# Two transformer blocks of a hybrid model, float32 by split products: the rows of the moving arrays get a pitch of 516 and 514 elements

## The chip, the cores and the metric

One core of a Trainium2 chip runs one program. The metric is the device time of that program in microseconds (us), from its start to its end. Before the change it was run twice: 3772.89 and 3775.09 us, median 3773.99 us.

## The reference

512 tokens of width 1024 go through two blocks of two layers each. Cut to what matters here, one layer of the first block is

```python
h = rms_norm(x, norm_mix[l]);  z = h @ w_in[l]
# attention, a gated recurrence (forward and backward) and a convolution of 31 taps, each on its part of z
x = x + concat([o_att, o_hg, o_cv]) @ w_out[l]
h = rms_norm(x, norm_mlp[l])
x = x + square(relu(h @ w_mlp_in[l])) @ w_mlp_out[l]      # 1024 -> 4096 -> 1024
```

A layer of the second block has the same frame with four mixers, a gate of width 1024 for each, a projection per mixer (512 to 1024) and one output projection, and then the same MLP. All of it is float32, so every large product is computed as three products of rounded parts.

## The kernel before, in words

**Layout.** Activations are kept transposed: partition p and row k of `xT` (128 x 8 x 512) hold feature 128k + p of all 512 tokens. The input of a projection is such an array, split in two of type fp32r (float32 as TensorE takes it in one pass): a high part, the value rounded (`hi = cast(y)`), and a low part, the rest (`lo = y - hi`). The pairs are

- `hH`, `hL` (lines 135 and 136): the normalised input of a layer and, later in the layer, the mixers' outputs, for all layers;
- `H2`, `L2` (lines 1147 and 1148; 1544 in the second block): the input of the MLP;
- `midH`, `midL` (lines 1145 and 1146; 1537 and 1538): the MLP's intermediate, 1024 of its 4096 features at a time;
- `yH`, `yL` (second block, four rows each): the output of one mixer.

Each is allocated by `sb`, which adds bytes behind a tile until its size is a multiple of 128 bytes. A row is 512 elements of 4 bytes, so every row begins 2048 bytes behind the one before it.

**Weights.** They come as a stream of units of 128 x 1024 elements. SyncE loads a unit into one of two slots of `w_raw` (line 257), ScalarE rounds it into `w_hi` (line 233, three slots), and GpSimd computes `w_lo = w_raw - w_hi` (line 280; VectorE does it for some units of the first block, line 249). ScalarE's rounding of a unit waits until the tile that used the slot three units earlier is done.

**Products.** `Group.part` (lines 322 to 345) takes one output tile of 128 features: for k from 0 to 7 it issues three matmuls into one PSUM bank, `w_hi` with the high row k (line 336), `w_lo` with the same high row (line 337), `w_hi` with the low row k (line 338). The activation row is the moving operand, 128 x 512; the weights, 128 x 128, are loaded anew ahead of each matmul. So a tile is 24 matmuls, and each of them reads one row of one moving array and nothing of the next row. `Group.some` (lines 308 to 310) does the same for the first two tiles of the output projection in the first block. Two PSUM banks alternate.

**Around it.** In the MLP the blocks `up0, down0, ... up3, down3` of eight tiles each follow one another. Behind an `up` tile VectorE does four operations in a row (`mlp_dve`, lines 506 to 510): max and scale out of PSUM, square, cast into `midH`, subtract into `midL`. Behind a `down` tile it adds to `xT` (line 371). `scale_dve` (lines 399 and 400) writes the pairs `hH`, `hL` and `H2`, `L2`; lines 1172, 1173, 1468, 1501, 1502, 2239 and 2240 write single rows of `hH` and `hL` from the mixers' outputs. Each of these instructions writes or reads one row as well. Order between engines is kept by semaphores written out by hand; none depends on an address.

Within a layer, arrays of different phases lie at the same addresses: the scopes of `midH`, `midL`, `H2`, `L2` are closed at once, and `Z` and others are laid over them.

Of the kernel before, what the change touches and what calls it, by code (L numbers as in the profile page):

```python
# [16 lines left out]
F32R = mybir.dt.float32r  # L17
# [7 lines left out]
P = 128  # L25
T = 512
NT = T // P
D = 1024
NK = D // P
# [76 lines left out]
def program(nc, given, out):  # L106
# [5 lines left out]
    with ctx:  # L112
        used = {}

        def sb(name, shape, dt=F32, scope=ctx):


            used[name] = used.get(name, 0) + 1
            name = f"{name}_{used[name]}"
            tile = scope.enter_context(nc.sbuf_tensor(name, shape, dt))  # L120
            rest = (-(int(np.prod(shape[1:])) * BYTES[dt]) // 32 * 32) % ALIGN
            if rest:
                scope.enter_context(nc.sbuf_tensor(f"{name}_pad", [P, rest], U8))
            return tile
# [7 lines left out]


        xT = sb("xT", [P, NK, T])
        hH = sb("hH", [P, NK, T], F32R)
        hL = sb("hL", [P, NK, T], F32R)
        rstd = sb("rstd", [P, T])
        w_raw = sb("w_raw", [P, 2, UNIT])
        w_hi = sb("w_hi", [P, WB, UNIT], F32R)
# [68 lines left out]
        def since(s):  # L208


            return begin.get(s.num, 0)
# [206 lines left out]
        def out_pe(layer, early, late, ready, out_tiles=None):  # L418


            begun = out_tiles is not None
            out_tiles = out_tiles or Group(layer, "out")
            for ks in (late,) if begun else (early, late):
                for tile in range(2):
                    out_tiles.some(tile, ks, ready, ks is early, ks is late)
            del out_tiles.tiles[0:2]
            out_tiles.products()
# [24 lines left out]
        def out_dve(layer, y, hi, lo, sq):  # L452
            add_and_scale(2 * layer + 1, Group(layer, "out"), y, hi, lo, sq)

        def h_ready(r):
            return lambda k: pe.wait_ge(h_split, NK * r + k + 1)
# [5 lines left out]

        def mlp_pe(layer, H2, L2, midH, midL, sq, behind=None):
            r = 2 * layer + 1
            for b in range(FB):
                Group(layer, f"up{b}", lambda nk: (H2, L2)).products(
                    ready=h_ready(r) if b == 0 else None,
                    sums=(lambda k: sum_squares(r, sq) if k == NK - 1 else None) if b == 0 else None)
                down = Group(layer, f"down{b}", lambda nk: (midH, midL))
                ready = lambda k, b=b: pe.wait_ge(mid_ready, since(mid_ready) + NK * b + k + 1)  # L470
                if b < FB - 1 or behind is None:
                    down.products(ready=ready)
                    continue
                for k in range(NK):
                    down.products(1, None if k else ready)
                    behind(k)
# [24 lines left out]
        def mlp_dve(layer, midH, midL, r_sb, y, sq, side=None):  # L501
            dve.wait_ge(rstd_ready, 2 * layer + 2)

            def hidden(i, a, free, value):
                r = r_sb[:, i % 2, :]
                dve.scalar_tensor_tensor(r, a[:, :], 0.0, rstd[:, :], ALU.max, ALU.mult).then_inc(up(free), 1)
                dve.wait_ge(free, value)
                link(dve, dve.tensor_tensor(r, r, r, ALU.mult))
                link(dve, dve.tensor_copy(midH[:, i, :], r))  # L509
                dve.tensor_tensor(midL[:, i, :], r, midH[:, i, :], ALU.subtract).then_inc(up(mid_ready), 1)  # L510
            for b in range(FB):
                Group(layer, f"up{b}").evacuate(hidden)
                down = Group(layer, f"down{b}")
                if b == FB - 1:
                    break
                for k in range(NK):
                    down.evacuate(add_to_x, 1)
                    if side and b == 1:
                        side(k)
            add_and_scale(2 * layer + 2, down, y, hH, hL, sq, layer < LAYERS - 1)  # L520
# [596 lines left out]
        def next_bounds_dve(vec):  # L1117

            for d, (first, second) in enumerate((("lb_f0", "lb_f1"), ("lb_b0", "lb_b1"))):
                last = dve.tensor_tensor(lb_gap[:, 0, 2 * d:2 * d + 2], vec[:, V1[second]:V1[second] + 2],  # L1120
                                         vec[:, V1[first]:V1[first] + 2], ALU.subtract)
            last.then_inc(up(bound_gap), 1)
            dve.wait_ge(bound_softplus, since(bound_softplus) + 1)
            link(dve, dve.scalar_tensor_tensor(lb_now[:, :, 0], lb_gap[:, 0, :], 0.0, lb_gap[:, 1, :],
                                               ALU.min, ALU.subtract))
            dve.tensor_tensor(lb_now[:, :, 1], lb_now[:, :, 0], lb_gap[:, 0, :], ALU.subtract)
# [9 lines left out]
        def first_layer(layer):  # L1136
# [3 lines left out]
            with scope:  # L1140
# [1 line left out]
                conv_u = sb("conv_u", [P, 2, T + 30], F32, scope)  # L1142
                conv_c = sb("conv_c", [P, 2, T], F32, scope)
                with ExitStack() as mlp_scope:
                    midH = sb("midH", [P, NK, T], F32R, mlp_scope)
                    midL = sb("midL", [P, NK, T], F32R, mlp_scope)
                    H2 = sb("H2", [P, NK, T], F32R, mlp_scope)
                    L2 = sb("L2", [P, NK, T], F32R, mlp_scope)
                    pair_r = sb("relu_sb", [P, 2, T], F32, mlp_scope)
                Z = sb("Z", [P, 20, T], F32, scope)  # L1150
                cum = sb("cum", [P, 2, 2, T + 1], F32, scope)
# [33 lines left out]
                def on_tensor():  # L1185
# [83 lines left out]
                    out_pe(layer, None, [3, 6, 7], out_ready, out_tiles)  # L1269
                    mlp_pe(layer, H2, L2, midH, midL, pair)  # L1270

# [99 lines left out]
                def on_vector():  # L1371
# [132 lines left out]
                    next_bounds_dve(vec)  # L1504
                    out_dve(layer, yt, H2, L2, pair)
                    mlp_dve(layer, midH, midL, pair_r, yt, pair, None if layer else angles_dve)
# [24 lines left out]
        def second_layer(layer):  # L1531
# [2 lines left out]
            scope = ExitStack()  # L1534
            with scope:
                with ExitStack() as s1:
                    midH = sb("midH2", [P, NK, T], F32R, s1)
                    midL = sb("midL2", [P, NK, T], F32R, s1)
                mixed = sb("mixed", [P, NK, T], F32, scope)
                yH = sb("yH", [P, 4, T], F32R, scope)  # L1540
                yL = sb("yL", [P, 4, T], F32R, scope)
                small = sb("small", [P, T], F32, scope)
                with ExitStack() as s1:
                    H2, L2 = sb("H2_2", [P, NK, T], F32R, s1), sb("L2_2", [P, NK, T], F32R, s1)
                    pair_r = sb("relu2", [P, 2, T], F32, s1)
                Z0 = sb("Z0", [P, 12, T], F32, scope)
                Z1 = sb("Z1", [P, 12, T], F32, scope)
# [85 lines left out]
                def turn_out_pe(k):  # L1633
                    pe.wait_ge(out_scaled, k + 1)
                    if k >= 2:
                        pe.wait_ge(out_copied, k - 1)
                    for t in range(NT):
                        ins = pe.transpose(turned_bank(k)[:, t * P:(t + 1) * P], yt[:, k % 2, t * P:(t + 1) * P], ident)
                    ins.then_inc(out_turned, 1)
# [65 lines left out]
                def on_tensor():  # L1705
# [149 lines left out]
                    for a in range(2):  # L1855
# [13 lines left out]
                    out_pe(layer, [0, 1, 2, 3], [4, 5, 6, 7], lambda k: pe.wait_ge(out_split, since(out_split) + k + 1))  # L1869
                    mlp_pe(layer, H2, L2, midH, midL, pair,  # L1870
                           (lambda k: turn_out_pe(k - 1) if 0 < k < NK - 1 else None) if final else None)
# [383 lines left out]
        for layer in range(DEPTH):  # L2255
            first_layer(layer)
        for layer in range(DEPTH, LAYERS):
            second_layer(layer)
# [137 lines left out]
```

## Time and profile before

| what | value |
|---|---|
| time, median of two runs | 3773.99 us |
| the two runs | 3772.89 and 3775.09 us |
| profiled execution, first to last instruction | 3772.8 us |
| what lies around that span (median less span) | 1.2 us |
| mean granted TensorE clock over the span | 0.980 of full speed |
| TensorE busy | 3647.3 us, 97% of the span |

The profile comes from one execution. Its span counts from the first instruction to the last; the device time of a run has a little more around it. "PE" is TensorE's matmuls, "PEld" its weight loads, which lie beside the matmuls, "DVE" VectorE, "ACT" ScalarE, "POOL" GpSimd. Matmuls are pipelined and the end of each is modelled, so the durations of neighbouring matmuls overlap: how fast they follow one another is read from their starts. The granted clock is given as a share of TensorE's 2.4 GHz.

### The profile page before, as it was taken

The page shows a single profiled execution, that of the slowest core. Times are in us where ns is not written, and L with a number is a line of the kernel's source. Part 1 is how long each engine was busy: PE and PEld are TensorE (multiplying, and loading weights), DVE is VectorE, ACT ScalarE, POOL GpSimd, SP SyncE. Part 2 cuts the span into 40 slices and gives each one's busy share as a digit, 9 for nine tenths or more (in the row PEclk, how much of TensorE's full clock was granted, in tenths as well). Part 3 has the DMA queues.
Part 4 walks back from the last instruction along what each step waited for, and adds up shares of the span by engine and source line. Part 5 has one row for each costly group of instructions (what it writes and reads, how often), then busy time and mean ns, then how long its engine had stood idle before and what let it go on. Part 6 is the DMA issues. An engine that isn't in the chain of part 4 may idle for free.

```text
span 3772.8 us, 44713 instructions
## 1 busy us (share of the span) xinstructions
PE 3647.3 (97%) x17876; PEld 2805.4 (74%) x17876; DVE 2131.7 (57%) x3000; ACT 1336.3 (35%) x2282; POOL 1195.8 (32%) x486
## 2 busy tenths in 40 slices
PE   8989999998999999999999999999999999999998
PEld 6646888865688878577777678887767777778887
DVE  7887565788655564633363585456553255365444
ACT  6354121534521132545333432122344433342212
POOL 0003444200244443132323244444213232334443
PEclk9989999998999999999999999999999999999999
DMA  4101333220133342021222133234112221223332
GB/s 139 40 12 62 97 99 95 90 63 12 45 95 95 97 140 81 29 79 56 78 62 73 56 91 99 95 95 148 46 45 73 62 79 62 65 73 94 99 95 84
DMA packets 80798, 292.39 MB, mean 77 GB/s; under 512 B 9648, under 2 KB 11088, under 8 KB 80080
## 3 DMA queue, kind: packets, MB, share of 16 engines
q1 hardware_dynamic: 77808, 278.49, 23.5%
q10 hardware_dynamic: 2784, 11.03, 0.9%
q8 instruction: 143, 2.34, 0.2%
q14 instruction: 63, 0.52, 0.0%
HBM read 285.30 MB, written 2.10 MB: 76 GB/s over the span
## 4 chain that ended last, share of the span: by engine, by line
PE 86%; DVE 9%; issue 2%; ACT 2%; DMA 0%; SPq 0%; DVEq 0%; ACTq 0%
PE acc L336 24%; PE acc L338 23%; PE acc L337 23%; PE banks L607 2%; PE banks L656 2%; PE banks L977 2%; PE banks L639 2%; PE banks L994 1%; PE banks L1731 1%; DVE stat L743 1%; DVE QK L892 1%; DVE conv_c L1396 1%; DVE near L920 1%; DVE pair L408 1%; PE banks L614 1%
## 5 line engine op out<-in xcount | busy, mean ns | idle before, releaser
L280 POOL TENSOR_TENSOR w_lo<-w_raw,w_hi 128x1024 fp32r<-128x1024 f32 x482 | 1195.6, 2481 | 2549.9 <-ACT w_hi L233 2549.9
L233 ACT ACTIVATE w_hi<-w_raw 128x1024 fp32r<-128x1024 f32 x518 | 549.0, 1060 | 1717.3 <-PE acc L338 1638.1
L336 PE MATMUL acc<-hH,w_hi 128*128 128x512 f32 x1776 | 729.7, 411 | 11.8 <-DVE sig L2119 6.6
L338 PE MATMUL acc<-hL,w_hi 128*128 128x512 f32 x1776 | 698.6, 393 | 0.0
L337 PE MATMUL acc<-hH,w_lo 128*128 128x512 f32 x1776 | 697.8, 393 | 0.0
L336 PEld LDWEIGHTS acc<-hH,w_hi 128*128 128x128 f32 x1776 | 337.3, 190 | 97.8 <-issue 25.7
L336 PE MATMUL acc<-H,w_hi 128*128 128x512 f32 x1024 | 400.5, 391 | 3.8 <-DVE L L400 3.8
L336 PE MATMUL acc<-midH,w_hi 128*128 128x512 f32 x1024 | 401.0, 392 | 0.3
L371 DVE TENSOR_TENSOR xT<-acc,xT 128x512 f32<-128x512 f32 x160 | 110.6, 692 | 511.3 <-PE acc L338 498.9
L337 PE MATMUL acc<-midH,w_lo 128*128 128x512 f32 x1024 | 398.7, 389 | 0.0
L338 PE MATMUL acc<-midL,w_hi 128*128 128x512 f32 x1024 | 398.6, 389 | 0.0
L338 PE MATMUL acc<-L,w_hi 128*128 128x512 f32 x1024 | 398.4, 389 | 0.0
L337 PE MATMUL acc<-H,w_lo 128*128 128x512 f32 x1024 | 398.4, 389 | 0.0
L338 PEld LDWEIGHTS acc<-hL,w_hi 128*128 128x128 f32 x1776 | 336.5, 189 | 73.1
L337 PEld LDWEIGHTS acc<-hH,w_lo 128*128 128x128 f32 x1776 | 337.5, 190 | 66.3 <-issue 4.3
L336 PEld LDWEIGHTS acc<-midH,w_hi 128*128 128x128 f32 x1024 | 192.2, 188 | 46.4 <-DVE midL L510 7.0
L336 PEld LDWEIGHTS acc<-H,w_hi 128*128 128x128 f32 x1024 | 192.2, 188 | 46.0 <-DVE L L400 5.5
L337 PEld LDWEIGHTS acc<-H,w_lo 128*128 128x128 f32 x1024 | 192.2, 188 | 40.7 <-issue 1.0
L338 PEld LDWEIGHTS acc<-midL,w_hi 128*128 128x128 f32 x1024 | 192.2, 188 | 40.3
L338 PEld LDWEIGHTS acc<-L,w_hi 128*128 128x128 f32 x1024 | 192.2, 188 | 40.0
L337 PEld LDWEIGHTS acc<-midH,w_lo 128*128 128x128 f32 x1024 | 192.3, 188 | 39.4
L509 DVE CAST midH<-relu 128x512 fp32r<-128x512 f32 x64 | 160.3, 2505 | 2.2
(338 smaller groups left out, 4720.3 us busy)
## 6 DMA issues: line engine op xcount, KB each, us to landing
w_raw<-in_stream SPq DMA_DIRECT2D x518, 512.0 KB, 3.6
cw<-in_cmpw ACTq DMA_DIRECT2D x2, 2048.0 KB, 7.5
mixed<-in_cmpw ACTq DMA_DIRECT2D x2, 2048.0 KB, 12.9
x_tok<-in_x SPq DMA_DIRECT2D x2, 1024.0 KB, 7.6
out<-probsT SPq DMA_DIRECT2D x4, 512.0 KB, 4.0
stack<-Z ACTq DMA_DIRECT2D x8, 128.0 KB, 2.3
stack<-Z ACTq DMA_DIRECT2D x8, 127.8 KB, 2.4
masks_f<-in_masks SPq DMA_DIRECT2D x1, 960.0 KB, 12.1
```

Of the source, the lines that this page charges most:

```text
L233: act.activation(w_hi[:, u % WB, 0:w], w_raw[:, u % 2, 0:w], ACT.Copy).then_inc(hi_split, 1)
L280: pool.tensor_tensor(w_lo[:, u % WB, 0:w], w_raw[:, u % 2, 0:w], w_hi[:, u % WB, 0:w], ALU.subtract)\
L336: pe.matmul(acc[n % 2][:, :], wh, H[:, k, :], start=(k == 0), stop=False)
L337: pe.matmul(acc[n % 2][:, :], wl, H[:, k, :], start=False, stop=False)
L338: last = pe.matmul(acc[n % 2][:, :], wh, Lo[:, k, :], start=False, stop=(k == nk - 1))
L371: dve.tensor_tensor(xT[:, i, :], a[:, :], xT[:, i, :], ALU.add).then_inc(up(free), 1)
L408: dve.tensor_tensor(sq[:, 0, :], sq[:, 0, :], sq[:, 1, :], ALU.add).then_inc(sq_added, 1)
L509: link(dve, dve.tensor_copy(midH[:, i, :], r))
L607: last = pe.matmul(self.score_banks[h % 3][:, 0:m], w["q"][r, qt * P:(qt + 1) * P], w["k"][r, lo * P:hi * P], start=True, stop=True, skip_ ...
L639: last = pe.transpose(self.turn_banks[n % 2][:, j * P:(j + 1) * P], self.P[:, s % 3, a, j * P:(j + 1) * P], ident)
L656: pe.matmul(self.out_bank[HD * a:HD * a + HD, cols], w["v"](kt, a), self.PT[:, a, kt, cols], start=(first and kt == 0), stop=True, skip_gr ...
L977: last = pe.matmul(scores, KK[r, jt * P:(jt + 1) * P], moving, start=(j == 0), stop=True, skip_group_check=True)
```

## The change

The six kinds of moving arrays of eight rows get longer rows: high parts 516 elements, low parts 514. The name is then bound to the first 512 elements of each row, so all code behind it is as before, and so is every instruction but for the addresses. `yH` and `yL` stay as they are.

```diff
@@ -132,8 +132,8 @@
         xT = sb("xT", [P, NK, T])
-        hH = sb("hH", [P, NK, T], F32R)
-        hL = sb("hL", [P, NK, T], F32R)
+        hH = sb("hH", [P, NK, T + 4], F32R)[:, :, 0:T]
+        hL = sb("hL", [P, NK, T + 2], F32R)[:, :, 0:T]
         rstd = sb("rstd", [P, T])
@@ -1142,10 +1142,10 @@
                 with ExitStack() as mlp_scope:
-                    midH = sb("midH", [P, NK, T], F32R, mlp_scope)
-                    midL = sb("midL", [P, NK, T], F32R, mlp_scope)
-                    H2 = sb("H2", [P, NK, T], F32R, mlp_scope)
-                    L2 = sb("L2", [P, NK, T], F32R, mlp_scope)
+                    midH = sb("midH", [P, NK, T + 4], F32R, mlp_scope)[:, :, 0:T]
+                    midL = sb("midL", [P, NK, T + 2], F32R, mlp_scope)[:, :, 0:T]
+                    H2 = sb("H2", [P, NK, T + 4], F32R, mlp_scope)[:, :, 0:T]
+                    L2 = sb("L2", [P, NK, T + 2], F32R, mlp_scope)[:, :, 0:T]
@@ -1534,14 +1534,14 @@
                 with ExitStack() as s1:
-                    midH = sb("midH2", [P, NK, T], F32R, s1)
-                    midL = sb("midL2", [P, NK, T], F32R, s1)
+                    midH = sb("midH2", [P, NK, T + 4], F32R, s1)[:, :, 0:T]
+                    midL = sb("midL2", [P, NK, T + 2], F32R, s1)[:, :, 0:T]
...
-                    H2, L2 = sb("H2_2", [P, NK, T], F32R, s1), sb("L2_2", [P, NK, T], F32R, s1)
+                    H2, L2 = sb("H2_2", [P, NK, T + 4], F32R, s1)[:, :, 0:T], sb("L2_2", [P, NK, T + 2], F32R, s1)[:, :, 0:T]
```

Row k of a high part now begins 2064k bytes behind the array's start, row k of a low part 2056k bytes. `hH` grows by 8 x 16 = 128 bytes per partition, `hL` by 64 and another 64 that `sb` adds, so what is allocated behind them begins 256 bytes later.

## Rows read from the trace of the kernel before

**Rows 1.** The page: busy time and the chain that ended last.

```profile
PE 3647.3 (97%) x17876; PEld 2805.4 (74%) x17876; DVE 2131.7 (57%) x3000; ACT 1336.3 (35%) x2282; POOL 1195.8 (32%) x486
...
PE 86%; DVE 9%; issue 2%; ACT 2%; DMA 0%; SPq 0%; DVEq 0%; ACTq 0%
PE acc L336 24%; PE acc L338 23%; PE acc L337 23%; PE banks L607 2%; PE banks L656 2%; PE banks L977 2%; PE banks L639 2%; PE banks L994 1%; PE banks L1731 1%; DVE stat L743 1%; DVE QK L892 1%; DVE conv_c L1396 1%; DVE near L920 1%; DVE pair L408 1%; PE banks L614 1%
```

**Rows 2.** Groups of instructions by line: matmuls that read the changed arrays.

```profile
L336 PE MATMUL acc<-hH,w_hi 128*128 128x512 f32 x1776 | 729.7, 411 | 11.8 <-DVE sig L2119 6.6 <-DVE yt L2141 3.3 <-DVE hL L400 1.9
L336 PE MATMUL acc<-midH,w_hi 128*128 128x512 f32 x1024 | 401.0, 392 | 0.3
L336 PE MATMUL acc<-H,w_hi 128*128 128x512 f32 x1024 | 400.5, 391 | 3.8 <-DVE L L400 3.8
L308 PE MATMUL acc<-hH,w_hi 128*128 128x512 f32 x64 | 26.0, 406 | 2.4 <-DVE hL L1502 2.4
```

**Rows 3.** Windows: an up block, a down block, two gate or output blocks.

```profile
core 0: us, PE busy (x) PEld busy (x) DVE busy (x) ACT busy (x) POOL busy (x), PEclk, DMA share, GB/s
439.00:482.50 43.50, 43.50 (x194) 36.03 (x193) 32.76 (x29) 8.50 (x8) 19.70 (x8) 1.00 0.30 97
482.50:526.30 43.80, 43.78 (x193) 35.94 (x192) 20.39 (x20) 12.22 (x12) 19.48 (x8) 1.00 0.29 97
1842.50:1864.30 21.80, 21.80 (x98) 18.06 (x97) 3.46 (x5) 6.09 (x7) 9.67 (x4) 1.00 0.32 99
2174.40:2217.90 43.50, 43.50 (x193) 36.02 (x192) 32.77 (x31) 18.26 (x23) 21.34 (x8) 1.00 0.29 86
```

**Rows 4.** Timeline of TensorE where an up block ends and a down block begins.

```profile
start us, us, engine line op out<-in xcount [idle before <-releaser]
482.02 0.39 PE L337 MATMUL acc<-H,w_lo 128*128 128x512 f32 x1
482.25 0.39 PE L338 MATMUL acc<-L,w_hi 128*128 128x512 f32 x1
482.47 0.39 PE L336 MATMUL acc<-midH,w_hi 128*128 128x512 f32 x1
482.70 0.39 PE L337 MATMUL acc<-midH,w_lo 128*128 128x512 f32 x1
482.93 0.39 PE L338 MATMUL acc<-midL,w_hi 128*128 128x512 f32 x1
483.15 0.39 PE L336 MATMUL acc<-midH,w_hi 128*128 128x512 f32 x1
```

**Rows 5.** Timeline of TensorE where a gate block ends and a mixer's projection begins.

```profile
1674.81 0.39 PE L338 MATMUL acc<-hL,w_hi 128*128 128x512 f32 x1
1675.04 0.39 PE L336 MATMUL acc<-yH,w_hi 128*128 128x512 f32 x1
1675.26 0.39 PE L337 MATMUL acc<-yH,w_lo 128*128 128x512 f32 x1
1675.49 0.39 PE L338 MATMUL acc<-yL,w_hi 128*128 128x512 f32 x1
```

**Rows 6.** Timeline of TensorE around the one wait of a down block.

```profile
487.01 0.39 PE L338 MATMUL acc<-midL,w_hi 128*128 128x512 f32 x1
487.41 0.50 PE L336 MATMUL acc<-midH,w_hi 128*128 128x512 f32 x1
487.75 0.39 PE L337 MATMUL acc<-midH,w_lo 128*128 128x512 f32 x1
```

**Rows 7.** Timeline of TensorE: matmuls of the unsplit form on arrays not changed.

```profile
1723.92 1.02 PE L1805 MATMUL banks<-soft_sb,C 128*128 128x512 f32 x2
1724.78 1.02 PE L1806 MATMUL banks<-soft_sb,C 128*128 128x512 f32 x2
1725.63 0.59 PE L1807 MATMUL banks<-soft_sb,C 128*128 128x256 f32 x2
```

**Rows 8.** VectorE by line (min/median/max ns): the convolution's taps, the MLP's operations.

```profile
L1396 DVE SCALAR_TENSOR_TENSOR conv_c<-conv_u,vec,conv_c x120: 717/747/753, 53.7 to 953.6; 128x512 f32<-128x512 f32 x120
L506 DVE SCALAR_TENSOR_TENSOR relu<-acc,rstd x64: 683/692/692, 2226.9 to 3713.4; 128x512 f32<-128x512 f32 x64
L509 DVE CAST midH<-relu_sb x64: 2496/2506/2506, 359.9 to 1338.2; 128x512 fp32r<-128x512 f32 x64
L510 DVE TENSOR_TENSOR midL<-relu_sb,midH x64: 691/693/693, 362.5 to 1340.7; 128x512 fp32r<-128x512 f32 x64
```

## The prediction

> **What bounds the kernel now.** I read the page's busy line and chain first, then the groups by line, then windows of single blocks, and last the timeline of TensorE. The page says that TensorE bounds the kernel: it is busy 97% of the span, 86% of the chain that ended last is its matmuls, and 70% of that chain are lines 336, 337 and 338, the split products [rows 1]. The groups give their number [rows 2]: line 336 reads `hH` 1776 times, `midH` 1024 times and the MLP's input `H` 1024 times, line 308 reads `hH` 64 times. Lines 337 and 338 (309 and 310) have the same counts, so 3 x (1776 + 1024 + 1024 + 64) = 11,664 matmuls read an array that the change touches. The 411, 392 and 391 ns in those rows are latencies that overlap; the rate has to come from windows and starts.
>
> The windows give it [rows 3]. An up block, 192 matmuls, takes 43.5 us: 226.6 ns from one start to the next. The window of gate products at 1842.5 us and the output projection at 2174.4 us come out the same, 21.8/96 = 227 and 43.5/192 = 226.6 ns. A down block takes 0.3 us more. All of this is at the granted clock 1.00, that is 2.4 GHz. So the matmuls in question hold 11,664 x 0.2267 = 2644 us, 70% of the span, which agrees with the chain. 512 columns at one column a cycle of 2.4 GHz are 213.3 ns; each matmul costs 13.3 ns more than that, 155 us over all 11,664. This is the only place where a row's address could give something back, and the reader should keep that number: it is the ceiling of any gain in the products.
>
> Does anything in the trace say that those 13.3 ns depend on addresses? Three readings say no. First, inside a block the starts are even. In [rows 4] they go 0.23, 0.22, 0.23, 0.23, 0.22 us, whether a matmul reads the same row as the one before it (336 to 337), the row of the same number in another array (337 to 338), or the next row (338 to 336). The step from `L` to `midH` at 482.25 to 482.47 us is one like the others, and so is the step from `hL` to `yH` at 1674.81 to 1675.04 us [rows 5]. Second, the arrays do not begin at the same place. Adding up the allocations, `H2` and `midH` of the first block begin 1536 bytes past a multiple of 2048 from `hH` (constants 5632, 1024 and 1920 bytes, vectors 768, `freq` 128, `conv_u` 4352 lie between, the rest are multiples of 2048), and `yH` begins at another offset; the weight slots are at 0. The rate is the same for all. Third, the rate does not feel the other engines: in the up block VectorE works 32.8 of 43.5 us and GpSimd 19.7, in the gate block only 3.5 of 21.8 and 9.7, and the rate is within 0.4 ns [rows 3]. The excess of the down block is one wait at its second tile, 0.40 and 0.34 us between starts instead of 0.23 [rows 6], where the last row of `midL` arrives a little late.
>
> **The change part by part.** It adds no instruction, no wait and no transfer, and removes none. Every instruction that reads or writes a changed array takes one row, which stays 512 contiguous elements; no instruction steps from one row to the next, so the pitch itself is never walked. What changes is where a row starts. Row k of a high part moves by 16k bytes, of a low part by 8k bytes, against the array's start. Before, every row began on a multiple of 128 bytes; afterwards only row 0 does. That touches 7/8 of the products, 10,206 matmuls. Of the low rows, every odd one starts 8 bytes past a multiple of 16: half of 3888, so 1944 matmuls.
>
> Products: the trace has no matmul of this form whose moving row starts off a multiple of 128 bytes, so the cost has to be bounded. From below: all of the 13.3 ns goes, 10,206 x 13.3 = 136 us. That this is a rate TensorE can have is seen in the unsplit form [rows 7]: two matmuls of line 1805 and two of 1806 take 1725.63 - 1723.92 = 1.71 us, 427.5 ns for 512 columns, which is two cycles a column (426.7) and 0.8 ns, with the weights changed each time. From above: the low rows off 16 bytes run at that slower rate, 427.5 - 226.7 = 201 ns more on 1944 matmuls, 390 us. These ends are far apart. The nearest row for a shifted start is on VectorE: the convolution's taps read `conv_u` at offsets of tap x 4 bytes in rows of 542 elements, so they start at every multiple of 4 bytes, and the 120 instructions take 717/747/753 ns, minimum, median and maximum [rows 8]. Their starts move through all offsets, and none is over 1% above the median, nor more than 4% below it. I take that value: 0 us for the products.
>
> VectorE's writes of the rows: `midH` and `midL` 128 times each, the other pairs fewer. By the taps, 0 again; were each of the some 500 operations 50 ns longer they would still lie in the 5.44 us that a tile of 24 matmuls takes. In the MLP the four operations take 692 + 692 + 2506 + 693 = 4.58 us a tile [rows 8], so 0.86 us is left. The exception is the last row of `midL`, which TensorE already waits for once per down block: 50 ns on two operations would show there, 16 x 0.1 = 1.6 us in all. Everything behind `hL` begins 256 bytes later; weights and scratch stay on multiples of 128 bytes, and the offsets compared above differ by more than that without any effect. 0 us.
>
> Sum: 3772.8 us of span, 1.2 us around it, 0 for each edit: 3774.0 us.
>
> The Trainium skill gives a figure that would speak for more ("TensorE: Matmul & The Clock Gate", on the back-to-back gap): 215.7 ns from one warm matmul of 512 columns to the next, in bfloat16. The trace has 226.7 here, so the page does not describe this form as it stands. If the start addresses were what keeps this kernel from it, 10,206 x 11.0 = 112 us would go and the time would be 3662 us.
>
> **The rivals.** *Starts that repeat modulo 128 bytes collide.* Each matmul streams its row while the next weights are read, 512 bytes per partition that begin on a multiple of 512. If the two streams meet in the same part of the memory because all start on multiples of 128, turning the starts would free them. For it: 13.3 ns is too regular for chance, it appears in this form and not in the unsplit one, and no row here starts off the grid, so nothing excludes it. Against it: the stream of activations runs through 2048 bytes while the weights' runs through 512, so they pass each other whatever the start. In full it gives 3774 - 136 = 3638 us, and nothing else takes over: a tile would take 24 x 213.3 = 5.12 us, still over VectorE's 4.58. It decides from 75.5/10,206 = 7.4 ns a matmul. The Trainium skill ("SBUF — State Buffer", on its two separate sides) says that engine-side contention happens only at the port pair shared by VectorE and GpSimd. By that rule this rival gives nothing; the even rate under a busy and an idle VectorE agrees.
>
> *A start off 16 bytes costs TensorE time.* The place is line 338 at odd k, `hL`, `L2` and `midL`. The price that the trace offers for a read which is less even is the taps' 747 ns against 692 ns of line 506, the same operation on aligned rows [rows 8]: 55 ns. On 1944 matmuls that is 107 us, and as TensorE is the bound, all of it reaches the end: 3881 us, slower. It decides from 39 ns on each of those matmuls. Against it: a quarter of the taps start on multiples of 16, and none of the 120 comes under 717 ns, so the 55 ns belong to the operation's operands and not to the offset.
>
> *A small price per shifted start.* One cycle of 2.4 GHz is 0.42 ns; on 10,206 matmuls 4.3 us per cycle. A read that touches one more piece of memory might cost a few. Seven cycles would be 30 us, in either direction. This stays within 2% and sets the range.
>
> That the change does not do what it says cannot be: the addresses do move. That moving them does nothing is the forecast.
>
> **How the numbers follow.** No change that can be measured, 3774 us: 0.81 together with the small price. The collision, 3638 us or at least 75 us less: 0.10. The start off 16 bytes, 3881 us or at least 75 us more: 0.09. A measurement of this kernel can tell about 2% from no change. The range reaches 30 us to each side, seven cycles for each shifted start, 3744 to 3804 us; both large rivals lie outside it, and they hold just under 2 in 10.
>
> **What would show it.** Right: an up block still takes 43.5 us, a down block 43.8, steps of 0.23 us at all k; the taps, the cast at 2506 ns and line 510 at 693 ns unchanged. For the collision: up blocks of 41 to 42 us, and steps that are shorter for k over 0 than for k = 0. For the price off 16 bytes: steps after line 338 longer at odd k alone, up blocks of over 44.8 us. The forecast is wrong if the block times move by over 2%, or if the time moves while they don't, which I have no mechanism for.

## The result: slower by 1.4%, and the profile after

The changed kernel takes 3827.47 us (two runs, 3827.45 and 3827.49) against 3773.99 us: ratio 1.0139, 95% interval 1.0122 to 1.0156. The predicted time was 3774 us with a range to 3804; the result is 53.5 us later and lies outside it. The profiled execution's span is 3826.1 us, 53.3 more than before.

The page after, busy time and the chain that ended last, beside [rows 1]:

```profile
PE 3702.0 (97%) x17876; PEld 2811.6 (73%) x17876; DVE 2125.4 (56%) x3000; ACT 1337.6 (35%) x2282; POOL 1197.3 (31%) x486
...
PE 86%; DVE 9%; issue 2%; ACT 2%; DMA 0%; SPq 0%; DVEq 0%; ACTq 0%
```

TensorE's busy time grew by 54.7 us with the same 17,876 matmuls. No other engine's moved by over 7 us, and the chain has the same shares. So no wait and no transfer has come in: the same matmuls run slower. The windows say which, in the order of [rows 3] (up block, down block, gate products, output projection), with one more behind them for a block of 48 matmuls that reads `yH` and `yL`, whose pitch was not changed:

```profile
core 0: us, PE busy (x) PEld busy (x) DVE busy (x) ACT busy (x) POOL busy (x), PEclk, DMA share, GB/s
443.70:488.10 44.40, 44.40 (x193) 36.03 (x192) 32.79 (x29) 8.51 (x8) 19.70 (x8) 1.00 0.31 92
488.10:532.80 44.70, 44.70 (x193) 35.99 (x193) 20.41 (x20) 12.23 (x12) 19.50 (x8) 1.00 0.31 96
1867.80:1890.10 22.30, 22.30 (x98) 18.07 (x97) 3.46 (x5) 6.09 (x7) 9.67 (x4) 1.00 0.32 97
2203.20:2247.70 44.50, 44.50 (x193) 36.06 (x192) 30.44 (x31) 18.29 (x23) 21.80 (x8) 1.00 0.29 84
...
1665.60:1676.60 11.00, 11.00 (x51) 9.13 (x50) 2.08 (x3) 3.30 (x6) 4.56 (x2) 1.00 0.20 60
```

An up block went from 43.5 to 44.4 us, a down block from 43.8 to 44.7, the gate products from 21.8 to 22.3, the output projection from 43.5 to 44.5: 231 to 232 ns a matmul instead of 226.7, at the same granted clock 1.00 and with the same work on the other engines beside it. The block on `yH` and `yL` takes 11.0 us, 229 ns a matmul with its restart, as before. Over a whole MLP the two traces differ like this, before:

```profile
356.60:701.10 344.50, 344.43 (x1515) 283.69 (x1514) 199.10 (x185) 80.23 (x83) 156.50 (x63) 1.00 0.31 95
```

and after:

```profile
359.70:711.20 351.50, 351.50 (x1515) 283.84 (x1514) 199.28 (x185) 80.33 (x83) 156.52 (x63) 1.00 0.31 93
```

Four layers with 7.0 us each are 28 us of the 53; the other 25 are left for the 5520 matmuls that read `hH` and `hL`.

The intervals are no longer even. The starts at the end of an up block, beside [rows 4]:

```profile
start us, us, engine line op out<-in xcount [idle before <-releaser]
486.99 0.39 PE L337 MATMUL acc<-H,w_lo 128*128 128x512 f32 x1
487.22 0.40 PE L338 MATMUL acc<-L,w_hi 128*128 128x512 f32 x1
487.45 0.39 PE L336 MATMUL acc<-H,w_hi 128*128 128x512 f32 x1
487.69 0.39 PE L337 MATMUL acc<-H,w_lo 128*128 128x512 f32 x1
487.91 0.40 PE L338 MATMUL acc<-L,w_hi 128*128 128x512 f32 x1
488.15 0.39 PE L336 MATMUL acc<-midH,w_hi 128*128 128x512 f32 x1
```

0.23, 0.23, 0.24, 0.22, 0.24 us. In nanoseconds of the trace the median intervals within a tile of an up block are, for k = 0 to 7 and lines 336, 337, 338: 232/229/234, 227/234/230, 235/231/234, 226/233/235, 229/232/237, 230/231/231, 234/226/237, 231/225/238. The pattern is the same in every tile, of `H2`, of `midH` and of `hH`, so it goes by addresses. It does not follow k's parity, and k = 0, whose high row did not move against the start of its array, is not spared.

VectorE's operations, beside [rows 8], are what they were:

```profile
L1396 DVE SCALAR_TENSOR_TENSOR conv_c<-conv_u,vec,conv_c x120: 717/747/752, 53.7 to 966.1; 128x512 f32<-128x512 f32 x120
L509 DVE CAST midH<-relu_sb x64: 2503/2507/2511, 363.0 to 1357.6; 128x512 fp32r<-128x512 f32 x64
L510 DVE TENSOR_TENSOR midL<-relu_sb,midH x64: 691/693/697, 365.6 to 1360.2; 128x512 fp32r<-128x512 f32 x64
```

### The profile page after: what moved, and what is told of

It reads as the page before. It is cut to its first block, busy times and chain, and to the rows that moved or that the text cites. A ratio compares the mean times of both kernels' runs of the same rounds, so it can differ in the third digit from the quotient of the medians.

```text
span 3826.1 us, 44713 instructions
## 1 busy us (share of the span) xinstructions
PE 3702.0 (97%) x17876; PEld 2811.6 (73%) x17876; DVE 2125.4 (56%) x3000; ACT 1337.6 (35%) x2282; POOL 1197.3 (31%) x486
## 4 chain that ended last, share of the span: by engine, by line
PE 86%; DVE 9%; issue 2%; ACT 2%; DMA 0%; SPq 0%; DVEq 0%; ACTq 0%
PE acc L336 24%; PE acc L338 23%; PE acc L337 23%; PE banks L607 2%; PE banks L656 2%; PE banks L977 2%; PE banks L639 2%; PE banks L994 1%; PE banks L1731 1%; DVE stat L743 1%; DVE QK L892 1%; DVE conv_c L1396 1%; DVE near L920 1%; DVE pair L408 1%; PE banks L614 1%
## 5 line engine op out<-in xcount | busy, mean ns | idle before, releaser
L336 PE MATMUL acc<-hH,w_hi 128*128 128x512 f32 x1776 | 737.4, 415 | 11.2 <-DVE sig L2119 6.3
L338 PE MATMUL acc<-hL,w_hi 128*128 128x512 f32 x1776 | 707.6, 398 | 0.0
L337 PE MATMUL acc<-hH,w_lo 128*128 128x512 f32 x1776 | 706.0, 398 | 0.0
L338 PEld LDWEIGHTS acc<-midL,w_hi 128*128 128x128 f32 x1024 | 192.3, 188 | 44.4
L338 PEld LDWEIGHTS acc<-L,w_hi 128*128 128x128 f32 x1024 | 192.3, 188 | 44.2
L509 DVE CAST midH<-relu_sb 128x512 fp32r<-128x512 f32 x64 | 160.4, 2507 | 2.2
```

The costliest lines, as they stand in the source:

```text
L336: pe.matmul(acc[n % 2][:, :], wh, H[:, k, :], start=(k == 0), stop=False)
L337: pe.matmul(acc[n % 2][:, :], wl, H[:, k, :], start=False, stop=False)
L338: last = pe.matmul(acc[n % 2][:, :], wh, Lo[:, k, :], start=False, stop=(k == nk - 1))
```

## The experiments

My theory after the result was that the start addresses of the rows cost TensorE time, in one of three forms: by each row's own place (theory A in the expectations), by the change of the place from one matmul to the next (theory P), or by the place against that of the weights, which are loaded while the row streams (theory W). All fourteen kernels compute the whole reference, with the same instructions; only addresses differ. Since a pair of arrays has blocks of its own in the trace, one kernel can hold several cases.

One thing has to be said ahead of them. The addresses given in each kernel's compiled program were read out only after the eighth run; they stand in no profile. In the kernel before, all moving arrays and the weight slots begin at 128 modulo 256. An array whose size is an odd multiple of 128 bytes moves everything behind it by 128 bytes against what lies ahead. So some kernels hold other offsets than their expectations say; below, "offset" is that of the moving row less that of the weights, modulo 256 bytes, from those addresses.

**1 and 2: one half of the change at a time.**

```diff
-        hH = sb("hH", [P, NK, T], F32R)
+        hH = sb("hH", [P, NK, T + 4], F32R)[:, :, 0:T]
         hL = sb("hL", [P, NK, T], F32R)
...
```

and the same for the other high arrays; the second kernel does it for the low ones, with T + 2.

> High parts at a pitch of 516, low parts at 512. Theory A (a row that starts off the 128-byte grid costs TensorE time, whatever lies before it): 7776 of 11,664 matmuls read high rows, 2/3 of the 53 us come, 3809 us. Theory P (what costs is the change of the start's offset from one matmul to the next): the step from one high row to the same high row keeps its offset, the steps to the low row and on to the next high row don't, and they change as often as in the changed kernel, so most of the 53 us come, 3815 to 3828 us, and the intervals of matmuls that follow such a step are the long ones.

> Low parts at a pitch of 514, high parts at 512. Theory A: 3888 matmuls read low rows, 1/3 of the 53 us, 3792 us; if only rows off 16 bytes cost (the second rival of the prediction), the whole 53 us would be here, 3827 us, and none in the kernel with high parts alone. Theory P: the offset changes twice per three matmuls as before, so 3810 to 3828 us.

High alone: 3824.78 us, ratio 1.0135 (1.012 to 1.015). Low alone: 3814.82 us, ratio 1.0108 (1.0092 to 1.0125). The loss is not shared out: 50.6 and 40.6 us, where both together make 53. Neither fits a price per row off the grid (3809 and 3792). The windows of an up block and a down block with high rows alone, and of an up block in the first and in the second block of layers with low rows alone:

```profile
444.70:489.30 44.60, 44.60 (x194) 36.05 (x193) 32.75 (x29) 8.49 (x8) 19.73 (x8) 1.00 0.32 95
489.30:533.80 44.50, 44.50 (x193) 35.94 (x192) 20.41 (x20) 12.21 (x12) 19.52 (x8) 1.00 0.32 95
```

```profile
442.30:486.50 44.20, 44.20 (x194) 36.06 (x193) 32.76 (x29) 8.50 (x8) 19.71 (x8) 1.00 0.31 93
2416.50:2461.10 44.60, 44.60 (x193) 36.07 (x192) 32.81 (x29) 8.49 (x8) 19.77 (x8) 1.00 0.31 96
```

The same code with the same pitch takes 44.2 us in one block and 44.6 in the other. By the addresses the offsets are 128 and 128 + 8k in the first, 0 and 8k in the second. These two kernels turned out to undo less than they seemed to, since `hH` with 516 elements a row is an odd multiple of 128 bytes, and so is `hL` with 514: both moved the weights.

**3: how large must the step be?**

```diff
-        hH = sb("hH", [P, NK, T], F32R)
-        hL = sb("hL", [P, NK, T], F32R)
+        hH = sb("hH", [P, NK, T + 2], F32R)[:, :, 0:T]
+        hL = sb("hL", [P, NK, T + 2], F32R)[:, :, 0:T]
...
-                    H2 = sb("H2", [P, NK, T], F32R, mlp_scope)
+                    H2 = sb("H2", [P, NK, T + 32], F32R, mlp_scope)[:, :, 0:T]
...
```

> High and low rows of one pair get the same pitch, and each pair another one: hH/hL +8 bytes, H2/L2 of the first block +128, midH/midL of the first block +64, H2/L2 of the second block +32, midH/midL of the second block +16. Only the step from the low row to the next high row changes the offset, by the pitch's excess. Both theories: the blocks with +128 bytes stay at 226.7 ns a matmul, so the pitch of 2048 bytes as such is nothing. Where the interval begins to rise (at +64, +32, +16 or +8) gives the unit of memory that counts. Theory A: up blocks with offsets off the unit take about 5 ns a matmul more. Theory P: one step of three changes, so 1.5 to 3 ns a matmul.

3826.27 us in one run. Every pair is slow. Up block with a step of 128 bytes, down block with 64, up block with 32:

```profile
445.20:489.80 44.60, 44.60 (x194) 36.02 (x193) 32.80 (x29) 8.49 (x8) 19.77 (x8) 1.00 0.31 95
489.80:534.50 44.70, 44.70 (x194) 36.00 (x193) 20.41 (x20) 12.21 (x12) 19.50 (x8) 1.00 0.33 95
2427.30:2472.00 44.70, 44.70 (x194) 36.05 (x193) 32.82 (x29) 8.50 (x8) 19.75 (x8) 1.00 0.30 95
```

Both theories had said that 128 bytes cost nothing. A row that starts on a multiple of 128 bytes, 16 or 64 is no better than one that starts 8 bytes past it. Whatever counts has a unit of over 128 bytes.

**4: whole arrays moved, pitch 512.**

```diff
-                    midH = sb("midH", [P, NK, T], F32R, mlp_scope)
+                    midH = sb("midH", [P, NK * T + 2], F32R, mlp_scope)[:, 2:NK * T + 2].rearrange("p (k t) -> p k t", t=T)
...
```

> Pitch 512 everywhere, but whole arrays begin off the grid: first block H2 and L2 both 16 bytes, midH and midL both 8 bytes; second block L2 alone 16 bytes (H2 at 0), midL alone 64 bytes; hH and hL unchanged as control. Theory A: up and down blocks of the first block rise from 43.5 to 44.5 us (231.7 ns a matmul) and those of the second by a third of that. Theory P: the first block's stay at 226.7 ns a matmul (43.5 us), since no offset changes from one matmul to the next, and the second block's up blocks rise, by 3 to 5 ns a matmul. Theory W (what counts is the offset against the weights, which start at 0): the first block's blocks change to one constant other interval, longer or shorter.

3810.99 us in one run. Up and down block of the first block of layers, an up block of the second, and the output projection on the unmoved `hH`:

```profile
442.60:487.00 44.40, 44.40 (x193) 36.01 (x193) 32.80 (x29) 8.50 (x8) 19.76 (x8) 1.00 0.32 95
487.00:532.00 45.00, 45.00 (x194) 36.19 (x193) 20.41 (x20) 12.22 (x12) 19.49 (x8) 1.00 0.32 95
2417.40:2462.00 44.60, 44.60 (x194) 36.07 (x193) 32.81 (x29) 8.49 (x8) 19.78 (x8) 1.00 0.30 94
2193.40:2236.90 43.50, 43.50 (x193) 36.04 (x192) 32.80 (x31) 18.26 (x23) 21.32 (x8) 1.00 0.30 86
```

A pitch of 2048 bytes does not protect: the moved arrays are slow, and only `hH` keeps 43.5 us. This kernel did not test theory P cleanly, since its low arrays had moved by another 128 bytes (offsets 16 and 144, 8 and 136).

**5: high and low row at one and the same offset.**

```diff
-                    midH = sb("midH", [P, NK, T], F32R, mlp_scope)
-                    midL = sb("midL", [P, NK, T], F32R, mlp_scope)
+                    midH_midL = sb("mid_pair", [P, 8194], F32R, mlp_scope)
+                    midH = midH_midL[:, 2:4098].rearrange("p (k t) -> p k t", t=512)
+                    midL = midH_midL[:, 4098:8194].rearrange("p (k t) -> p k t", t=512)
...
```

> Pitch 512; high and low array of a pair lie in one tile, so that both begin at the same offset, and that offset is not 0: first block H2/L2 16 bytes, midH/midL 8 bytes; second block H2/L2 64, midH/midL 128. hH/hL stay at 0. Theory P (only a change of the offset from one matmul to the next costs, whatever the offset is): all blocks at 226.7 ns a matmul, time as before, 3774 us. Theory A (off the grid costs) and theory W (the offset against the weights counts): blocks of the first block at 230 to 235 ns, 3790 to 3815 us.

3805.86 us in one run. The pairs lie at offsets 144 (not 16) for the first `H2`, 8, 64 and 128, and `hH` at 0:

```profile
440.50:485.30 44.80, 44.80 (x193) 36.19 (x192) 32.74 (x29) 8.50 (x8) 19.64 (x8) 1.00 0.30 93
485.30:530.30 45.00, 45.00 (x194) 36.23 (x193) 20.36 (x20) 12.20 (x12) 19.41 (x8) 1.00 0.31 97
...
2193.40:2236.90 43.50, 43.50 (x194) 36.03 (x193) 32.75 (x31) 18.27 (x23) 21.34 (x8) 1.00 0.30 86
```

The second block's up blocks at offset 64 take 43.9 us (2327.7 to 2371.6), its down blocks at 128 take 44.8 (2371.6 to 2416.4). No offset changes from one matmul to the next inside these blocks. Three of the four kinds are at least as slow as in the changed kernel, the fourth is slow by 0.4 us. So theory P has fallen as the whole cause.

**6 and 7: the weights moved instead.**

```diff
-        w_hi = sb("w_hi", [P, WB, UNIT], F32R)
-        w_lo = sb("w_lo", [P, WB, UNIT], F32R)
+        w_both = sb("w_both", [P, 3200 + WB * (UNIT + 4)], F32R)
+        w_hi, w_lo = (w_both[:, at:at + WB * (UNIT + 4)].rearrange("p (u t) -> p u t", t=UNIT + 4)[:, :, 0:UNIT] for at in (0, 3200))
```

```diff
-        w_lo = sb("w_lo", [P, WB, UNIT], F32R)
+        w_lo = sb("w_lo", [P, WB * UNIT + 4], F32R)[:, 4:WB * UNIT + 4].rearrange("p (u t) -> p u t", t=UNIT)
```

> The activations lie as in the kernel before; the three slots of w_hi and of w_lo get a pitch of 1028 elements, so their weights begin at 0, 16 and 32 bytes past the grid, w_lo as w_hi. Theory W: tiles of the three slots run at different rates, those at 16 and 32 bytes at up to 5 ns a matmul more. Theory P (offset of the moving rows alone): all at 226.7 ns, at most a few matmuls longer where a tile changes slot.

> Activations as before, w_hi as before, w_lo begins 16 bytes further, so that of three weight loads in a row one starts at another offset. If TensorE's two reads are alike and it is a change of offset that costs, in either of them, 230 to 235 ns a matmul everywhere, 3815 to 3850 us. Theory P for the moving rows alone: 226.7 ns, 3774 us.

3823.74 and 3834.38 us, one run each. In both, all that is allocated behind the weights moved by another 128 bytes (the MLP's arrays are at offsets 96 to 128), which the expectations left out; `hH` and `hL` did not move. In the sixth kernel two tiles of the first projection follow one another, both on `hH` and `hL` as they were; the first one's weights lie in the slot moved by 16 bytes, the second one's in that moved by 32:

```profile
61.39:66.84 5.45, 5.45 (x26) 4.50 (x24) 5.38 (x8) 5.32 (x9) 0.00 (x0) 1.00 0.33 99
66.84:72.43 5.59, 5.59 (x25) 4.51 (x24) 5.52 (x8) 5.46 (x9) 0.00 (x0) 1.00 0.26 75
```

5.45/24 = 227 and 5.59/24 = 233 ns. Moving rows that have not moved at all are read at the slow rate once the weights lie elsewhere. That leaves theory W, the offset between the two. But the first of the two tiles is at offset 240, not 0, and it is fast, as is every other undisturbed tile on `hH` in that slot (25 of them, 227.0 ns; at offset 224 all are at 233). So 16 bytes off is not slow in itself.

In the seventh kernel the matmuls on `hH` and `hL` alternate between offset 0 and, with w_lo, 240, two offsets that are fast when they stand alone. The output projection takes 44.6 us, 232.2 ns a matmul. A change of offset from one matmul to the next can thus cost as well: of theory P this much is left. And it need not cost. Eight tiles of the first projection in the first layer, and the same eight in the second layer, with the same offsets:

```profile
39.92:84.51 44.59, 44.59 (x194) 36.04 (x192) 37.06 (x48) 31.88 (x44) 0.00 (x0) 1.00 0.30 91
733.09:776.61 43.52, 43.52 (x194) 36.05 (x193) 37.05 (x48) 32.00 (x44) 0.00 (x0) 1.00 0.27 89
```

232.2 and 226.7 ns a matmul, each held over all eight tiles. The offset alone does not fix the rate.

**8: the unit.**

> Pitch 512, the high array at 0 and the low one further by: first block H2/L2 128 bytes, midH/midL 256; second block H2/L2 512, midH/midL 1024. In the kernel with equal steps a pitch excess of 128 bytes gave 232 ns with a pattern that came back after four rows, 512 bytes. Theory P with a unit of 512 bytes: 230 to 235 ns at 128 and 256, 226.7 at 512 and 1024. With a unit of 2048 bytes: all four longer. With one of 128 bytes: all four 226.7.

The edit is that of experiment 5, with the high array at 0 and the low one 128, 256, 512 and 1024 bytes further. 3777.56 us in one run. Up block with 128, down block with 256, output projection unchanged:

```profile
440.20:484.10 43.90, 43.90 (x193) 35.97 (x192) 32.81 (x29) 8.50 (x8) 19.75 (x8) 1.00 0.32 95
484.10:527.90 43.80, 43.78 (x193) 35.95 (x192) 20.39 (x20) 12.22 (x12) 19.48 (x8) 1.00 0.32 97
2177.90:2221.40 43.50, 43.50 (x193) 36.04 (x192) 32.77 (x31) 18.26 (x23) 21.34 (x8) 1.00 0.29 86
```

At 256 bytes a down block takes its old 43.8 us; at 1024 one takes 43.9 (2354.4 to 2398.3), and at 512 an up block takes 43.5 (2310.9 to 2354.4). Only 128 bytes cost, 43.9 us, and there the long interval is the one behind line 338, 234 ns, with 226 and 227 behind the other two. The unit is 256 bytes.

**9 and 10: offset against the weights, or a place of its own?**

```diff
+        sb("gap", [P, 32])
         w_hi = sb("w_hi", [P, WB, UNIT], F32R)
```

```diff
+        ctx.enter_context(nc.sbuf_tensor("first", [P, 32], U8))
         xT = sb("xT", [P, NK, T])
```

> Pitches as in the kernel before; 128 bytes are left free ahead of w_hi, so that weights and everything behind them (H2, L2, midH, midL, yH, yL) begin at 0 modulo 256 and hH, hL, which lie ahead, stay at 128. Theory W (what counts is the offset of the moving row against the weights that are loaded meanwhile, modulo 256): MLP blocks and yH/yL at 226.7 ns a matmul, blocks that read hH/hL (5520 matmuls) at 229 to 233 ns, 3787 to 3808 us. Theory A (the moving row's own offset counts, 128 modulo 256 is good): hH/hL at 226.7 and the MLP at 232, 3800 to 3810 us.

> Pitches as in the kernel before; 32 bytes are left free ahead of everything, so that every array and the weights begin at 160 modulo 256 instead of 128. Theory W: all blocks at 226.7 ns, time as before, 3774 us. Theory A: all blocks at about 232 ns, 3825 to 3835 us.

The ninth: 3797.84 us, ratio 1.0062 (1.0045 to 1.0079). Up block, down block, output projection:

```profile
444.30:487.80 43.50, 43.50 (x193) 36.05 (x192) 32.82 (x29) 8.51 (x8) 19.77 (x8) 1.00 0.32 96
487.80:531.70 43.90, 43.88 (x194) 35.99 (x193) 20.42 (x20) 12.22 (x12) 19.51 (x8) 1.00 0.32 97
2189.10:2233.90 44.80, 44.80 (x194) 36.05 (x193) 30.49 (x31) 18.26 (x23) 21.89 (x8) 1.00 0.28 84
```

The MLP's arrays moved by 128 bytes together with the weights and kept 43.5 us. `hH` did not move, and its projection went to 44.8 us, 233 ns a matmul. This is the run that decides between theories W and A: theory A had it the other way round. It also gives a price of the blocks on `hH` alone, 23 us, near the 25 left over above, though at another offset. The tenth: 3775.65 us in one run, with everything at 160 modulo 256, and

```profile
440.70:484.20 43.50, 43.50 (x194) 36.04 (x193) 32.76 (x29) 8.50 (x8) 19.68 (x8) 1.00 0.31 96
2176.00:2219.50 43.50, 43.50 (x194) 36.03 (x193) 32.73 (x31) 18.27 (x23) 21.32 (x8) 1.00 0.29 87
```

the old rates. At offset 0 no place is good or bad in itself.

**11: the changed kernel with all array starts at one offset.**

```diff
-ALIGN = 128
+ALIGN = 256
```

> The changed kernel (pitches 516 and 514) with every array rounded up to 256 bytes instead of 128, so that hL, midL and L2 begin at the weights' offset and not 128 bytes off it. Only the pitch is left: high rows 16k, low rows 8k bytes against the weights. If the lengthened rows alone make the loss: 230 to 232 ns a matmul and 3815 to 3828 us; if the 128 bytes of the low arrays' starts made a good part of it: 227 to 229 ns, 3780 to 3800 us.

3817.31 us, ratio 1.011 (1.0095 to 1.0126); an up block takes 44.3 us and the output projection 44.4:

```profile
444.20:488.50 44.30, 44.30 (x193) 36.07 (x192) 32.82 (x29) 8.51 (x8) 19.75 (x8) 1.00 0.30 93
2194.50:2238.90 44.40, 44.40 (x194) 36.13 (x193) 30.53 (x31) 18.27 (x23) 21.87 (x8) 1.00 0.27 86
```

So about 42.5 of the changed kernel's 53.5 us come with the rows' steps alone. The remaining 11, by difference, go with the 128 bytes by which `hL`, `midL` and `L2` had moved against the weights, a side effect of the padding. This part is weakly shown: the two intervals (from 1.0122 and up to 1.0126) just overlap, a tile's mean interval falls only from 231.7 to 231.1 ns, which is 7 us over 11,664 matmuls, and arrays outside the products moved too.

**12 and 14: is any offset faster than 0?** The edits are those of experiments 5 and 6 together.

> Pitch 512. The three slots of w_hi and w_lo begin 0, 64 and 128 bytes past the old offset; of the moving pairs hH/hL lie 0 bytes past it, H2/L2 of the first block 32, midH/midL of the first block 96, H2/L2 of the second block 16, midH/midL of the second block 8. So each pair is read against three offsets: 0, 192, 128 (hH, yH); 32, 224, 160; 96, 32, 224; 16, 208, 144; 8, 200, 136 bytes modulo 256. Theory W: the rate of a tile goes by the slot of its weights; 226.7 ns only at 0; equal differences (32 and 224 appear in two pairs) give equal rates. A difference at which a matmul takes less than 226.7 ns would be a kernel faster than both.

> Pitch 512. The weights' slots begin 8, 24 and 40 bytes past the old offset, the moving pairs 0 (hH/hL), 48 (first block H2/L2), 80 (first block midH/midL), 112 (second block H2/L2) and 176 bytes (second block midH/midL), so the differences modulo 256 are 248, 232, 216; 40, 24, 8; 72, 56, 40; 104, 88, 72; 168, 152, 136. Theory W as found so far: every tile at 228 to 236 ns. If the two reads only have to be out of each other's way and 0 is one such place among several, one of these differences runs at 226.7 ns or less.

3831.58 and 3801.01 us, one run each. Three tiles of the first projection in the twelfth kernel, at offsets 0, 192 and 128:

```profile
55.94:61.38 5.44, 5.44 (x25) 4.50 (x24) 5.41 (x8) 4.64 (x8) 0.00 (x0) 1.00 0.23 86
61.38:66.98 5.60, 5.60 (x26) 4.51 (x24) 5.53 (x8) 5.47 (x9) 0.00 (x0) 1.00 0.23 69
66.98:72.56 5.58, 5.58 (x26) 4.52 (x25) 5.51 (x8) 5.45 (x9) 0.00 (x0) 1.00 0.32 91
```

The rate changes from tile to tile with the slot of the weights: 226.7, 233 and 232.5 ns. In the fourteenth, three tiles of one up block, at 40, 40 and 8 bytes:

```profile
447.66:453.24 5.58, 5.58 (x26) 4.53 (x25) 4.18 (x4) 1.07 (x1) 2.07 (x1) 1.00 0.33 92
464.29:469.73 5.44, 5.44 (x25) 4.50 (x24) 4.18 (x4) 1.07 (x1) 2.07 (x1) 1.00 0.28 74
475.18:480.77 5.59, 5.59 (x25) 4.51 (x24) 4.18 (x4) 1.06 (x1) 2.08 (x1) 1.00 0.34 102
```

The first two have the same offset, weight slot and moving array and the same neighbours on the other engines, and yet 232.5 and 226.7 ns. Over the whole kernel 15 of 20 undisturbed tiles of the first block's `H2` at offset 40 are fast, and all 21 of `midH` at the same offset are at 231.9. Offset 24 ran at 227 ns in that block as well. So 0 is not the only offset at which the fast rate occurs, but it is the one at which nearly every undisturbed tile of every kernel here had it, and no tile was faster than 226.6 ns. As far as TensorE's rate goes, none of these kernels beats the one before.

The fourteenth kernel shows one thing more. It is the only one whose `w_hi` and `w_lo` begin 8 bytes past a multiple of 16, and in it GpSimd's subtraction into `w_lo` (line 280) takes 2004 ns at the median instead of 2405, and VectorE's cast into `midH` (line 509), which runs beside it, 2107 instead of 2506. TensorE is busy as long as in experiment 11 (3691.5 and 3690.6 us), and the span is 13.5 us shorter (3799.7 and 3813.2). So an address can also give time back, on another engine. Which of the operands does it is open, and a kernel that has these weight addresses together with offset 0 was not run.

**13: longer rows that keep the offset.**

```diff
-                    midH = sb("midH", [P, NK, T], F32R, mlp_scope)
+                    midH = sb("midH", [P, NK, T + 64], F32R, mlp_scope)[:, :, 0:T]
...
```

> H2, L2 in both blocks and midH, midL in the first get a pitch of 576 elements, 2304 bytes, so that the rows are lengthened and yet every row begins at the weights' offset modulo 256; the other arrays as before. Theory W: these blocks stay at 226.7 ns a matmul (up blocks of 43.5 us) and the time at 3774 us. If a pitch other than 2048 bytes costs by itself, or the unit is larger than 256 bytes: 231 to 233 ns in these blocks and 3790 to 3800 us.

3774.96 us in ten runs against 3774.87 in thirteen: ratio 1.000 (0.9991 to 1.001).

```profile
441.00:484.50 43.50, 43.50 (x193) 36.02 (x192) 32.76 (x29) 8.50 (x8) 19.69 (x8) 1.00 0.33 98
484.50:528.40 43.90, 43.88 (x193) 35.97 (x193) 20.39 (x20) 12.21 (x12) 19.48 (x8) 1.00 0.32 97
```

A pitch of 2304 bytes is as good as one of 2048. The change lost by its 16 and 8 bytes a row and the 128 bytes of the starts, not by leaving the power of two.

## Why the prediction was wrong

**What bounds the kernel: right.** TensorE was the bound, 11,664 matmuls at 226.7 ns were the place where a row's address could act, and what they lost reached the end: 11,664 x 5.0 ns = 58 us by the mean interval after (231.7 ns), 53 us measured. The 5 us of difference are shared: the MLPs lost 28 where 6144 x 5.0 = 31, the blocks on `hH` 25 where 5520 x 5.0 = 28. Behind a wait the kernel before was not at 226.7 ns either.

**The failing step: "I take that value: 0 us for the products".** The term was bounded between -136 and +390 us and set to 0 by VectorE's taps. What it measured is +5.0 ns a matmul on average over all 11,664, 12 cycles of 2.4 GHz. The taps are right about VectorE and say nothing of TensorE. They too read two rows at once, `conv_u` at a moving start and `conv_c` at a fixed one, and lost nothing; TensorE, which streams a row while the next weights are loaded, did. The nearest row was near by its words (a shifted start) and came from another engine.

**The step that let it pass: the second reading.** It said that "the arrays do not begin at the same place" and that the rate is the same for all. The sum of allocations behind it was wrong, since it left out `lb_now`, `lb_gap` and `refs`, 512 bytes: in the program `hH`, `H2` and `midH` of the first block all begin at 128 modulo 2048, those of the second block at 1920. And a right sum would not have helped, since every one of these places is 128 modulo 256, like the weights. The trace before held one offset only, 0. The evidence from `L` to `midH` and from `hL` to `yH` [rows 4, 5] was one case seen many times. The first rival names this gap for 128 bytes ("nothing excludes it"), but the forecast went on as if it were closed.

**The first rival, collision of the two streams:** it named the quantity that the runs support, the start of the moving row against that of the weights, and its sign was wrong. The common offset was not where they collide but where they run best. That they "pass each other whatever the start", its counter-argument, has fallen with experiments 6 and 9: the start matters.

**The rival of a start off 16 bytes:** wrong. Steps of 128, 64 and 32 bytes cost as much (experiment 3), and the intervals behind line 338 are long at even k too (234, 234, 237 and 237 ns). Its 107 us were twice the loss.

**The small price per shifted start** was the nearest to the size: it reached to 7 cycles and 30 us where 12 cycles came, averaged over all matmuls and not over 7/8 of them. Its range is what the result fell out of. Its form was wrong too, since it went by the row's own place.

**The other terms: right.** VectorE's operations and the tiles behind `hL` cost nothing by themselves; that everything behind moved by 256 bytes was harmless because it is 256. But `hL`, `midL` and `L2` themselves moved by 128 against the weights, which the sum did not have: 7 to 11 us by experiment 11.

The sentence from the Trainium skill ("SBUF — State Buffer", on its two separate sides), that on the engines' side only the port pair shared by VectorE and GpSimd causes contention, was used to give the first rival nothing. It does not cover this case: the changed kernel differs only in addresses, and TensorE's rate changed with no other engine's work changed. Whether what it loses is contention between its own two reads is not shown.

**Open:** what happens inside TensorE. The runs show that the rate depends on the offset between moving row and weights modulo 256 bytes, and experiments 7 and 14 that it depends on something besides, since the same offsets ran at two rates within one kernel. Behind a wait the first five to eight intervals are uneven at offset 0 too (236, 229, 232, 231 ns among them), before they settle at 226.7. That looks like a rhythm between the two reads which holds or doesn't; this was not tested. Where the 13.3 ns over 512 cycles come from is open as well.

## What to carry to other kernels

In products of this kind (fp32r, new weights for each matmul), keep the moving rows and the weights at the same start modulo 256 bytes; where a row has to be padded, pad it to a multiple of 256 bytes, and round array sizes to the same, since one odd size moves everything behind it. An argument that addresses don't matter needs a case in the trace with a different address: compute the offsets modulo 128, 256 and 512 before counting arrays as different cases, and read them from the compiled program rather than from a sum. An analogy from another engine is weak, even where that engine makes two reads as well.

## What the runs showed of the hardware that was not expected

- A stream of fp32r matmuls, 128 x 512 with new weights each, takes 226.7 ns a matmul when moving row and weights start at the same place modulo 256 bytes, and 229 to 235 ns at most other offsets (up and down blocks of 43.9 to 45.0 us instead of 43.5 and 43.8). Offsets 240 (experiment 6) and 24 (experiment 14) ran at 227.0 ns.
- Off 0, the same offsets can hold either rate for many tiles on end: 232.2 ns over eight tiles and 226.7 ns over the same eight a layer later (experiment 7).
- The unit is 256 bytes: low rows 256, 512 or 1024 bytes further cost nothing, 128 bytes cost 2.2 ns a matmul if only the low rows have it (43.9 us an up block) and 5 to 7 if all have (44.8 us a down block in experiment 5, 44.8 us the output projection in experiment 9).
- At offset 0 the place itself does not matter: everything at 128, at 160 or, for the MLP, at 0 modulo 256 gives the same rate.
- GpSimd's subtraction of 128 x 1024 elements took 2004 ns instead of 2405 in the one kernel whose `w_hi` and `w_lo` begin 8 bytes past a multiple of 16 (experiment 14).
